# Normalizing attention rows inside the transposing product instead of in a pass on POOL

## The reference, cut to what matters

```python
# forgetting attention, for each block of 128 queries
logits = jnp.einsum('bhqd,bhkd->bhqk', qb, kb) + (cum[..., q0:kend, None] - cum[..., None, :kend])
logits = jnp.where(causal, logits, NEG_INF)
p = jax.nn.softmax(logits, axis=-1).astype(v.dtype)
outs.append(jnp.einsum('bhqk,bhkd->bhqd', p, vb))
# dilated attention, for each block
p = jnp.exp(s - m)
den = jnp.sum(p, axis=-1, keepdims=True)
o = jnp.einsum('bhqk,bhqkd->bhqd', (p / den).astype(v.dtype), vv)
# memory attention
p = jax.nn.softmax(s, axis=-1)
o = jnp.einsum('bhsm,bmhd->bshd', p.astype(vm.dtype), vm)
```

## Time and profile before

| | |
|---|---|
| median of 3 timed runs | 2861.29 us (2856.5 to 2867.2) |
| span of the profiled execution, first to last instruction | 2863.9 us |
| TensorE busy | 2580.2 us, 90% |
| VectorE busy | 1157.0 us, 40% |
| ScalarE busy | 801.4 us, 28% |
| POOL busy | 161.5 us, 6% |
| attention in A, first score product to last value product | about 218 to 341 us |
| attention in the two layers | about 1164 to 1322 us and 2089 to 2247 us |

### The profile page before, as it was taken

One profiled execution on the slowest core, in us unless ns is written; L12 is line 12 of the kernel. 1 busy time (PEld: TensorE's weight loads), 2 busy tenths in 40 slices (PEclk: granted clock), 3 DMA queues, 4 the chain that ended last, 5 costly groups with the idle time before them and its releaser, 6 DMA issues.

```text
span 2863.9 us, 30233 instructions
## 1 busy us (share of the span) xinstructions
PE 2580.2 (90%) x11744; PEld 1956.3 (68%) x11744; DVE 1157.0 (40%) x1664; ACT 801.4 (28%) x1110; POOL 161.5 (6%) x165
## 2 busy tenths in 40 slices
PE   5899886899999489999997999978999999799996
PEld 3674464677777258666875888856866787588885
DVE  5635564000000431354346655333135434655533
ACT  3432313010000142233233433313223323433331
POOL 0001100000000100331000000000033100000000
PEclk8995596899999789899998999989989999899998
DMA  6535041688888413101221222221210122122221
GB/s 238 191 117 206 1 179 50 254 317 319 316 313 311 185 54 117 41 7 59 89 103 45 102 97 95 103 75 67 103 48 1 70 93 88 59 94 98 103 89 45
DMA packets 55809, 353.75 MB, mean 124 GB/s; under 512 B 6016, under 2 KB 6656, under 8 KB 19328
## 3 DMA queue, kind: packets, MB, share of 16 engines
q1 hardware_dynamic: 40464, 294.67, 27.8%
q10 hardware_dynamic: 8640, 30.08, 2.8%
q0 software_dynamic: 6576, 27.26, 2.4%
HBM read 319.49 MB, written 32.51 MB: 123 GB/s over the span
## 4 chain that ended last, share of the span: by engine, by line
PE 44%; issue 40%; DVE 4%; POOL 2%; ACT 2%; DMA 1%; POOLq 0%; DVEq 0%; ACTq 0%
PE lin L870 9%; PE lin L629 7%; PE lin L630 6%; PE lin L643 5%; PE lin L882 5%; PE attn L729 3%; PE score L704 2%; PE trans L715 2%; PE lin L634 2%; POOL y L1861 1%; DVE rstd L1375 1%; PE sums L674 1%; PE sums L669 1%; PE score L701 1%; PE lin L807 0%
## 5 line engine op out<-in xcount | busy, mean ns | idle before, releaser
L629 PE MATMUL lin<-h_r,ring_r 128*128 128x512 f32 x1584 | 626.7, 396 | 46.5 <-ACT h_r L1053 35.7
L630 PE MATMUL lin<-h_r,ring_r 128*128 128x512 f32 x1584 | 622.0, 393 | 0.0
L1505 DVE TENSOR_TENSOR ring_r<-ring,ring_r 128x2048 fp32r<-128x2048 f32 x138 | 316.2, 2292 | 559.1 <-ACT ring_r L1049 559.0
L629 PEld LDWEIGHTS lin<-h_r,ring_r 128*128 128x128 f32 x1584 | 301.0, 190 | 123.7 <-ACT h_r L1053 31.0
L643 PE MATMUL lin<-low_r,ring_r 128*128 128x512 f32 x1392 | 350.1, 391 | 1.9
L630 PEld LDWEIGHTS lin<-h_r,ring_r 128*128 128x128 f32 x1584 | 301.4, 190 | 62.0
L1049 ACT CAST ring_r<-ring 128x2048 fp32r<-128x2048 f32 x138 | 262.4, 1902 | 166.1 <-PE lin L634 105.5
L643 PEld LDWEIGHTS lin<-low_r,ring_r 128*128 128x128 f32 x1392 | 261.3, 188 | 63.2 <-DVE low_r L1511 9.8
L870 PEld LDWEIGHTS lin<-y,ring 128*128 128x128 f32 x2304 | 262.6, 194 | 11.0 <-issue 11.0
L870 PE MATMUL lin<-y,ring 128*128 128x128 f32 x2304 | 263.0, 277 | 2.1 <-DVE y L1741 1.1
L1327 ACT ACTIVATE ob<-lin,lvec 128x512 f32<-128x512 f32 x88 | 68.7, 781 | 301.6 <-PE lin L643 243.7
(11 more groups left out here) (287 smaller groups left out, 3151.5 us busy)
## 6 DMA issues: line engine op xcount, KB each, us to landing
ring<-in_weights SPq DMA_DIRECT2D x281, 1024.0 KB, 4.9
slots_in<-nab POOLq DMA_DIRECT2D x1, 13312.0 KB, 42.6
y<-slots_in ACTq DMA_DIRECT2D x20, 512.0 KB, 3.6
slots_out<-ob ACTq DMA_DIRECT2D x18, 512.0 KB, 8.7
nab<-in_na_bias ACTq DMA_DIRECT2D x12, 448.0 KB, 3.3
slots_out<-nab POOLq DMA_DIRECT2D x1, 3072.0 KB, 48.4
x<-in_xT ACTq DMA_DIRECT2D x1, 2048.0 KB, 10.9
outT<-x POOLq DMA_DIRECT2D x1, 2048.0 KB, 6.6
```

The source lines that it names most:

```text
L629: pe.matmul(acc, wh, high(k), start=(k == 0), stop=False)
L630: mm = pe.matmul(acc, wl, high(k), start=False, stop=False)
L1505: dve.tensor_tensor(ring_r[:, slot, :], ring[:, slot, :], whole(ring_r[:, HIGH_SLOT[ph.name][c], :]), ALU.subtract).then_inc(*w_low.on(ph, c))
```

## The change

POOL's pass over the rows goes. VectorE makes a diagonal matrix of the inverse sums, identity times the column, right after the reciprocal (into one of two buffers, `diag`), and `turn` multiplies the block with this matrix instead of transposing it by the identity: the block is the stationary operand, so the product is the transposed block with each column scaled by its row's inverse sum. `turn` waits for the signal `diag_ready` where it waited for `p_ready`. The operation is an ordinary matmul, where before it was the transposing kind. On POOL only the bias additions are left in the layers, one after the other, each as soon as its table is there.

```diff
+        nab_all = nab[:, :, :].rearrange("p a b -> p (a b)")
+        diag = {"A": [nab_all[:, 1408 + i * P:1408 + (i + 1) * P] for i in range(2)],
+                "L": [tmp[:, 0, i * P:(i + 1) * P] for i in range(2)]}
...
-        p_ready = signal("p_ready", **tiles)
+        diag_ready = signal("diag_ready", **tiles)
...
                     if c0 == 0:
-                        pe.wait_ge(*p_ready.by(ph, i))
+                        pe.wait_ge(*diag_ready.by(ph, i))
                     if j >= 1:
                         pe.wait_ge(*pt_ready.by(ph, j - 1))
                     for c in range(n):
-                        mm = pe.transpose(trans[:, 0, c * P:(c + 1) * P],
-                                          probs[name][i % 3][:, (c0 + c) * P:(c0 + c + 1) * P], ident)
+                        mm = pe.matmul(trans[:, 0, c * P:(c + 1) * P], probs[name][i % 3][:, (c0 + c) * P:(c0 + c + 1) * P],
+                                       diag[name][i % 2], start=True, stop=True)
                     mm.then_inc(*t_done.on(ph, j))
...
                     dve.reciprocal(stat[:, 2, i % 4:i % 4 + 1], stat[:, 1, i % 4:i % 4 + 1]).then_inc(*rden_ready.on(ph, i))
+                    dve.wait_ge(*rden_ready.by(ph, i))
+                    dve.tensor_scalar(diag[name][i % 2], ident, stat[:, 2, i % 4:i % 4 + 1], None,
+                                      ALU.mult).then_inc(*diag_ready.on(ph, i))
...
-            def attention(ph, extra=None):
-                for i, (kind, hp, half, t) in enumerate(TILES[ph.name]):
-                    if extra:
-                        extra(i)
-                    n = key_chunks(kind, t) * P
-                    p = probs[ph.name][i % 3][:, 0:n]
-                    pool.wait_ge(*rden_ready.by(ph, i))
-                    pool.tensor_tensor(p, p, stat[:, 2, i % 4:i % 4 + 1].to_broadcast([P, n]),
-                                       ALU.mult).then_inc(*p_ready.on(ph, i))
...
-                def next_bias(i):
-                    if i == 0:
-                        bias(0)
-                    if i % TT == 2 and i // TT + 1 < NA_HEADS:
-                        bias(i // TT + 1)
-                attention(ph, extra=next_bias)
+                for hd in range(NA_HEADS):
+                    bias(hd)
```

More of the change, by code:

```diff
@@ L1871, in _ @@
                            zeros.unsqueeze(1).to_broadcast([P, 2 * MAX_TRIPS - 2, D])).then_inc(zeros_out, 16)
-            attention(A)
             pool.wait_ge(*route_ready.by(A, "slots"))
```

## The result

The changed kernel took 2905.34 us (2901.9 to 2905.4) against 2863.43 (2856.5 to 2867.2) before: a ratio of 1.0146 with a 95% interval of 1.0127 to 1.0165, 42 us slower. The forecast was 2898, between 2875 and 2920.

What follows compares the result with a forecast made beforehand. TensorE was taken to bound all three attention stages. Layers +32.4 and first block +4.4 us gave +36.8, taking the 2863.9 us span to 2900.7; timed median 2.6 lower, 2898, range 2875 to 2920.

Steps and rivals of the forecast that it cites:

- Bound, block cost: Attention stages: TensorE busy nearly everywhere; each transposed block costs 0.112 us more at full clock, 0.2125 at half.
- Layers, +16.2 forecast: Attention in each layer: 176 blocks add 19.7 us, less 3.5 absorbed in waits: +16.2, or +32.4 for two.
- I count 3.5 of the 5.1 us as absorbed: Mostly dilated tiles: longer products hide 3.5 of each layer's 5.1 us of TensorE waits for VectorE's copy.
- The diagonal, priced at nothing: VectorE, every tile: diagonal takes 0.25 us, 32 us in all, covered by idle time, so price nothing.
- What goes with POOL: 128 POOL multiplications, some 115 us, vanish and stop slowing VectorE; the dilated chain gets 0.43 us shorter.
- the 7 us that the prediction named as possible: Layers: POOL's twelve bias additions could hold diagonals through shared ports, at most 7 us; the sum has 0.
- The clock in A, +4.4 forecast: First attention block (A): +17.0 us at half clock throughout; a quarter of the stage at high clock leaves +4.4.
- leave the low level at times, and to fall back: First attention block (A): clock rises at times, falls back at the 8-row products and at the small tiles.
- The sum: Whole kernel: 32.4 for the layers plus 4.4 for the first block, +36.8 us; forecast 2898.
- 1: Rival, chance 0.07: fuller products raise the first block's clock, -33.4 us there, cancelling the layers' +32.4; about 2855.
- 3: Rival, chance 0.04: a product costs no more than a transpose, only POOL and VectorE work changes; -3 us, about 2859.
- 2: Rival, chance 0.08: VectorE becomes late in memory and dilated tiles, 0.41 us each, 20 us; 2918.

Runs made afterwards that it cites:

- n1: Changed kernel with neither diagonal nor POOL pass, rows unnormalized, blocks transposed by the identity: 2856.9 us, ratio 0.9985 to the kernel before.
- n2: Changed kernel with neither diagonal nor POOL pass, rows unnormalized, blocks multiplied by the identity as plain f32 products: 2897.3 us, ratio 1.0116 to the kernel before.
- e1: Kernel before, with the diagonal also made on VectorE and awaited but unused; POOL still normalizes, blocks still transposed: 2924.1 us, ratio 1.0222.
- e4: Changed kernel in the two layers only; first block A keeps POOL's pass and transposes of the kernel before: 2897.3 us, ratio 1.0121.
- f1: Kernel before, with the gate product of first block A on 128 rows, 120 of them zero, instead of 8: 2855.4 us, ratio 0.9976.
- f2: Changed kernel, with the gate product of first block A on 128 rows instead of 8: 2887.5 us, ratio 1.0091 to the kernel before.
- e2: Kernel before, with transposes replaced by plain f32 products with the identity; POOL still normalizes, no diagonal: 2896.6 us, ratio 1.0126.
- g1: Kernel before, with the normalizing multiplication on ScalarE instead of POOL, one tile late; transposes kept: 2856.9 us, ratio 0.9976.
- h1: f1 plus 32 f32 products nobody reads in first block A, and an added wait before A's attention: 2834.8 us, ratio 0.9895 to the kernel before.
- e3: Changed kernel with transposes put back; diagonal made and awaited but unused, no POOL pass, rows unnormalized: 2886.1 us, ratio 1.0067 to the kernel before.

## Why the prediction was right

**Bound, block cost.** Right in kind: TensorE binds in all three stages, a transpose is one instruction and an f32 product two. The size was a little low. The prediction added one instruction at the experts' rate, 0.112 us; the loop shows 0.125, for all eight run at 0.114 and the four at 0.1025. Over 176 blocks that is 22.0 us a layer, not 19.7.

**Layers, +16.2 forecast, +18.1 measured: the mis-sized term.** The pair n1 and n2 with the two kernels splits the 18.1 of a layer into -1.9 (POOL's pass gone), +17.3 (products), +2.7 (diagonal). The step that failed is the term "I count 3.5 of the 5.1 us as absorbed": TensorE's waits for the copied block fell from 5.1 only to 2.6. The line of the same view in the first layer after, and in n2:

```profile
PE trans L719 <- DVE y L1481: 2.6, 7, 0.8
```

```profile
PE trans L718 <- DVE y L1477: 0.3, 1, 0.3
```

Without the diagonal the longer products absorb nearly the whole wait, more than was forecast. It is the diagonal that brings 2.3 us of it back. The prediction had let POOL's departure pay for it, 0.43 us against 0.25 in a dilated tile. The steps of these tiles show 0.33 gained (5.97 before, 5.64 in n1) and 0.33 lost again (5.92 in n2, 6.25 after).

By kind of tile: neighborhood 73.8 to 83.1, +9.3 where 96 x 0.112 = 10.8 was forecast; dilated 43.7 to 46.4, +2.7 for 5.4 - 3.5 = 1.9; memory 40.4 to 46.4, +6.0 for 32 x 0.112 = 3.6. The last is the largest miss: 32 x 0.125 = 4.0, the 1.3 of the diagonal, and 0.7 not traced further. The neighborhood tiles came out below, though their block cost more than forecast, for the entry at the low level is shorter. From the scores of the third tile to those of the fourth it took 5.18 us before, at the low level, and 3.39 after, at the high one. Window of the changed kernel's first layer:

```profile
1170.20:1183.60 13.40, 11.13 (x31) 6.38 (x30) 7.47 (x18) 4.68 (x10) 2.09 (x1) 0.50 0.28 101
```

13.4 us, where it was 17.0.

**The diagonal, priced at nothing.** It was estimated at 0.25 us of VectorE's queue; it lasts 0.286 and adds 0.32. That the idle time of VectorE covers it holds in the neighborhood tiles (83.1 in n2 and after). It fails in the dilated and memory tiles, 5 us over the two layers, and that it is free in A is not shown. The idle time is there on average, but not in the dilated chain and not behind a table load of ScalarE, and an average cover hid that.

**What goes with POOL.** Right: the minimum is at 160 ns, and n1 shows 1.6 us gained in the dilated tiles of a layer (43.7 to 42.1). The forecast had 8 x 0.43 = 3.4 of it in the chain.

In e1 the diagonal, 286 ns alone, took 1022 ns on average in the layers and up to 1.59 us. The Trainium skill (SBUF — State Buffer, Who interferes with whom) says that tensor_scalar can take the ports shared with GpSimd and that the later of the two then blocks fully. e1's lengths agree. As to who is later: the diagonal was held where POOL started within 52 ns of it, even though the trace puts the diagonal's start first, and not where POOL started 125 ns or more behind. In the changed kernel only the bias additions could do it. No diagonal there was longer than 289 ns, and only two of the twelve additions touch one, at its edge: one starts 0.16 us after a diagonal, the other ends 0.04 us into one. So the 7 us that the prediction named as possible were not paid, and the case itself hardly arose.

**The clock in A, +4.4 forecast.** Measured +8.2 in the profiled pair, +6 to 7 by e4. The mechanism was right, and so was the share. The forecast's sum does a quarter of A's work at the high level, 0.25 x 90 = 22.5 us of its 127.8, and that is 18% of the time; a clock of 0.59 is 18% too. What was too small is the stage around it: TensorE's waits for the copied block in A are 5.6 us where they were 2.9. The line of before:

```profile
PE trans L715 <- DVE ob L1474: 2.9, 3, 1.4
```

That is 2.7 of the 3.8 us by which the forecast fell short; that they are the cause is not isolated, and the rest is not traced. Windows of the changed kernel within A:

```profile
240.00:258.00 18.00, 18.00 (x52) 10.77 (x50) 9.18 (x28) 3.20 (x9) 0.00 (x0) 0.50 0.62 254
260.00:263.00 3.00, 2.98 (x17) 1.72 (x16) 2.21 (x8) 0.71 (x2) 0.00 (x0) 1.00 0.00 0
265.50:272.30 6.80, 6.80 (x27) 5.04 (x26) 4.32 (x14) 2.17 (x8) 0.00 (x0) 0.50 0.00 0
```

The stage leaves the low level for a few microseconds, as "leave the low level at times, and to fall back" had it. That the 8-row products have to do with the fall f1 and f2 make likely, for with 128 rows the clock stays up longer. They are not all of it: in f2 it still falls once, at 302.6 us.

**The sum.** In the profiled pair: 0.8 ahead of A, 8.2 in A, -4.2 between A and the first layer, 18.1, -1.1, 18.1, -0.1: 39.8, and the spans differ by 39.6. The -4.2 had no place in the forecast; the experts' first product stands at 520.3 us in place of 514.9, 5.4 later instead of 9.0, so work behind A has some slack. It happened to stand against the two terms that were too small, some 4 us in A and 4 in the two layers, and that the total came out 7 us from the forecast and not 12 is luck.

**Rivals.** 1 came about in a small part only; 3 is refuted by e2. 2, VectorE late, came about by some 5 of its 20 us, in the tiles that it named.

Left open: whether transposes count as activity for the clock. f1 lifted A's clock with every transpose in place, so they do not hold it at the low level throughout by themselves, but no run changes them alone at equal work. Open too is what of n1's 6.2 us lies outside attention: its gap between the layers and its tail are 1.5 and 1.7 us shorter.

## What to carry to other kernels

Price a replaced TensorE operation by its instruction count and the distance of starts, not by the mean duration: an f32 product is two instructions where an f32 transpose is one. A pass on an engine that waits anyway cost little here (6 to 7 us, n1 and g1), so folding it into the bound engine gives away what that engine pays; if it disturbs VectorE, another idle engine is the place for it. Cover for an added instruction is to be read at the latest tile, behind table loads and handoffs, not from the mean idle time. And a stage whose clock moves between two levels needs more than one profiled execution before its length is compared: f1's and f2's happened to be their fastest.

## What the runs showed of the hardware

- TensorE's granted clock in A rose when its products were made fuller. With the same instructions, 8 rows made 128 took it from 0.51 to 0.67 (f1's profiled execution, its fastest). With 32 useless f32 products more, and a changed wait before the stage, it was 0.88, with 36 us less of busy time than before (h1).
- A VectorE tensor_scalar from SBUF to SBUF that starts together with a GpSimd multiplication lasts as long as that one: 1.59 us beside 1.47, and 0.286 alone. Where the multiplication started 125 to 138 ns after it (8 of 128), it kept its 0.29 us.
- Making one VectorE instruction per tile (e1) cost TensorE its clock in the layers, 0.86 for 0.95, and so more than the waits alone; without POOL's pass (e3) times of 2863 to 2877 and of 2886 to 2888 us stand beside each other, and the one with a trace, of the upper group, lost it for 20.5 us in each layer. n1, which differs from e3 only in that the diagonal is neither made nor awaited, stayed within 2854.6 to 2861.5 in ten executions.
